# Second block's attention scores: split and stacked halves through DRAM in place of 64-row fp32

## The reference, cut to what matters

```python
# fox: 8 heads of width 64, causal, with a cumulative forget term
logits = einsum('bhqd,bhkd->bhqk', qi, k) / sqrt(64) + ci[..., :, None] - c[..., None, :]
logits = where(kpos <= qpos, logits, -inf);  out = softmax(logits) @ v

# differential: 4 heads, each with two maps of width 64; q and k are rotated first (rope)
p = softmax(where(kpos <= qpos, q_m k_m^T / sqrt(64), -inf))   # m = 0, 1
out = (p[0] - lam * p[1]) @ v                                   # v has width 128
```

## Time and profile before

| | us |
|---|---|
| median of 3 runs (lowest, highest) | 2890.78 (2885.82, 2891.13) |
| profiled execution, its time | 2890.61 |
| profiled execution, its span | 2888.9 |
| PE busy | 2612.1 (90% of the span) |
| DVE, ACT, POOL busy | 1001.0, 722.6, 708.0 |
| mean granted PE clock | 0.942 |

### The profile page before, as it was taken

How to read it: one execution, slowest core, us unless ns; L and a number is a source line. 1 busy time by engine, 2 the same in 40 slices (tenths; PEclk the granted TensorE clock), 3 DMA queues, 4 the chain that set the end, 5 groups by cost and what they waited for, 6 DMA issues and landing times. The chain is left out here.

```text
span 2888.9 us, 32486 instructions
## 1 busy us (share of the span) xinstructions
PE 2612.1 (90%) x12846; PEld 2094.6 (73%) x12846; DVE 1001.0 (35%) x1466; ACT 722.6 (25%) x1057; POOL 708.0 (25%) x437
## 2 busy tenths in 40 slices
PE   5899997599739899999999989899999989996987
PEld 4677776599737688888888768577777766674876
DVE  4055524444343521312213340122322314555523
ACT  3134454122111210201001210343432014443012
POOL 2111113133323233433333312111101221110221
PEclk9999998699869899999999989899999999998998
DMA  4411111222221111111111113011102111112422
GB/s 159 88 33 37 37 38 57 53 68 61 74 73 43 38 50 51 44 51 51 44 51 51 36 37 109 24 44 44 45 30 95 38 31 44 44 44 73 146 72 89
DMA packets 229584, 165.92 MB, mean 57 GB/s; under 512 B 40081, under 2 KB 212919, under 8 KB 228704
## 3 DMA queue, kind: packets, MB, share of 16 engines
q1 hardware_dynamic: 217888, 135.01, 16.6%
q10 hardware_dynamic: 11584, 29.36, 2.8%
HBM read 125.50 MB, written 38.85 MB: 57 GB/s over the span
## 5 line engine op out<-in xcount | busy, mean ns | idle before, releaser
L253 POOL CAST Wh<-Wraw 128x1024 fp32r<-128x1024 f32 x155 | 162.8, 1050 | 1784.9 <-PE PS L301 772.3
L255 POOL TENSOR_TENSOR Wl<-Wraw,Wh 128x1024 fp32r<-128x1024 f32 x155 | 399.3, 2576 | 22.3
L282 PE MATMUL PS<-XAh,Wh 128*128 128x512 f32 x520 | 165.7, 400 | 8.3 <-POOL Wl L255 4.2
L282 PE MATMUL PS<-XAl,Wh 128*128 128x512 f32 x520 | 161.5, 392 | 0.0
L282 PE MATMUL PS<-XAh,Wl 128*128 128x512 f32 x520 | 161.0, 391 | 0.0
L282 PE MATMUL PS<-XBl,Wh 128*128 128x512 f32 x520 | 160.1, 389 | 0.0
L282 PE MATMUL PS<-XBh,Wh 128*128 128x512 f32 x520 | 160.1, 389 | 0.0
L282 PE MATMUL PS<-XBh,Wl 128*128 128x512 f32 x520 | 160.0, 389 | 0.0
L282 PE MATMUL PS<-Fh,Wh 128*128 128x512 f32 x512 | 157.6, 389 | 0.0
L282 PE MATMUL PS<-Fl,Wh 128*128 128x512 f32 x512 | 157.6, 389 | 0.0
L282 PE MATMUL PS<-Fh,Wl 128*128 128x512 f32 x512 | 157.6, 389 | 0.0
(11 more groups left out here) (377 smaller groups left out, 5065.3 us busy)
## 6 DMA issues: line engine op xcount, KB each, us to landing
Wraw<-in_w_in SPq DMA_DIRECT2D x67, 512.0 KB, 4.0
Wraw<-in_w_ffn_in SPq DMA_DIRECT2D x32, 512.0 KB, 4.1
Wraw<-in_w_ffn_out SPq DMA_DIRECT2D x32, 512.0 KB, 3.9
x_scr<-hT SPq DMA_DIRECT2D x2, 4096.0 KB, 12.9
Wraw<-in_w_out SPq DMA_DIRECT2D x16, 512.0 KB, 4.6
gate_scr<-gbuf ACTq DMA_DIRECT2D x16, 512.0 KB, 2.6
gin<-gate_scr ACTq DMA_DIRECT2D x8, 1024.0 KB, 7.3
xtok<-in_x SPq DMA_DIRECT2D x4, 1024.0 KB, 8.6
```

Source lines behind the costliest of these rows:

```text
L253: pool.tensor_copy(Wh[:, slot], Wraw[:, slot])
L255: pool.tensor_tensor(Wl[:, slot], Wraw[:, slot], Wh[:, slot].bitcast(F32), ALU.subtract).then_inc(w_ready, 1)
L282: mm = pe.matmul(PS[:, 2 * slot + b, :], w[:, slot, k], x[:, b * 512:(b + 1) * 512], start=(c == 0 and m == 0), stop=(c == len(xs) - 1 and ...
```

## The change

The query of each head is split in a high and a low half, which are stacked on 128 rows (high on rows 0 to 63, low on 64 to 127). The key is split too, and each half is duplicated on both row groups. Two fp32r matmuls replace the fp32 one: stacked query times key-high, and stacked query times key-low. The halves are moved between partitions by a store to DRAM and a load from it.

```diff
+        st_h, st_l = sb("st_h", [P, 2, S], F32R, R + 48), sb("st_l", [P, 2, S], F32R, R + 56)
+        qs_scr, ks_scr = dram("qs_scr", [2, 4, P, S]), dram("ks_scr", [2, 4, P, S])
+        def store_halves(eng, j, hi, lo, out_sem):
+            scr = qs_scr if j < 4 else ks_scr
+            eng.dma_start(scr[0, j % 4], hi.bitcast(F32)).then_inc(out_sem, 16)
+            eng.dma_start(scr[1, j % 4], lo.bitcast(F32)).then_inc(out_sem, 16)
+        def load_map(eng, g, bufs, in_sem):
+            at = g * HD * S
+            q, kh, kl = bufs
+            eng.dma_start(q[:].bitcast(F32), bass.AP(qs_scr.tensor, at, [[4 * P * S, 2], [S, HD], [1, S]])).then_inc(in_sem, 16)
+            eng.dma_start(kh[:].bitcast(F32), bass.AP(ks_scr.tensor, at, [[0, 2], [S, HD], [1, S]])).then_inc(in_sem, 16)
+            eng.dma_start(kl[:].bitcast(F32), bass.AP(ks_scr.tensor, at + 4 * P * S, [[0, 2], [S, HD], [1, S]])).then_inc(in_sem, 16)
+        def map_scores(pe, bufs, i, dst):
+            q, kh, kl = bufs
+            for c, w in pieces(i):
+                for x in (kh, kl):
+                    mm = pe.matmul(dst(c)[:, 0:w * P], q[:, i * P:(i + 1) * P], x[:, c * 512:c * 512 + w * P],
+                                   start=(x is kh), stop=(x is kl and c != i // 4))
+            return pe.matmul(dst(c)[:, (w - 1) * P:w * P], identb[:], diagb[:], start=False, stop=True)
...
 act_phase9, for each of the 13 tiles:
-                if j < 12:
-                    act.activation((Qa, Ka, VaT)[j // 4][:, j % 4], pair(n % 2), ACT.Copy, scale=-0.125 if j < 4 else 1.0
-                                   ).then_inc(ps_free, 1)
+                if j < 8:
+                    if j >= 2:
+                        act.wait_ge(qk_out[j % 2], 32 * (j // 2))
+                    act.activation(st_h[:, j % 2], pair(n % 2), ACT.Copy, scale=-0.125 if j < 4 else 1.0).then_inc(qk_hi, 1)
+                    act.wait_ge(qk_hi, j + 1)
+                    act.wait_ge(qk_lo, j + 1)
+                    store_halves(act, j, st_h[:, j % 2], st_l[:, j % 2], qk_out[j % 2])
...
 dve_phase9, after ms_done 4:
-            for k in range(KT):
-                ins = dve.scalar_tensor_tensor(hT[:, k], hT[:, k], pv[:, V_FIN + k:V_FIN + k + 1], pair(2), ALU.mult, ALU.mult)
-            ins.then_inc(h_final, 1)
+            for j in range(8):
+                dve.wait_ge(qk_hi, j + 1)
+                dve.scalar_tensor_tensor(st_l[:, j % 2], pair((N_FOX + j) % 2), -0.125 if j < 4 else 1.0,
+                                         st_h[:, j % 2].bitcast(F32), ALU.mult, ALU.subtract).then_inc(qk_lo, 1)
+                dve.wait_ge(qk_lo, j + 1)
+                dve.sem_inc(ps_free, 1)
+                for k in (2 * j, 2 * j + 1):
+                    if k < KT:
+                        ins = dve.scalar_tensor_tensor(hT[:, k], hT[:, k], pv[:, V_FIN + k:V_FIN + k + 1], pair(2),
+                                                       ALU.mult, ALU.mult)
+                if j == 3:
+                    ins.then_inc(h_final, 1)
...
 sp_phase10: waits for qk_out, and behind the two constants:
+            for h in range(2):
+                load_map(sp, h, fox_bufs[h], qk_in[h])
...
 sp_phase11 (sp_phase14 likewise, with b_s and load_head):
-            load_range(sp, N_ZA + 2, N_QB + 2)
+            todo = [((i - 1) * FOX_STEPS / len(FOX_FILL), "tile", N_ZA + 2 + i) for i in range(len(FOX_FILL))]
+            todo += [(FOX_STEPS * (h - 1) / H8, "head", h) for h in range(2, H8)]
+            for _, what, x in sorted(todo):
+                if what == "tile":
+                    load_range(sp, x, x + 1)
+                else:
+                    sp.wait_ge(f_s, NT * (x - 1))
+                    load_map(sp, x, fox_bufs[x % 2], qk_in[x % 2])
...
 pe_phase11, scores(u) (pe_phase14 likewise, for each of the two maps):
+                if i == 0:
+                    pe.wait_ge(qk_in[h % 2], 48 * (h // 2 + 1))
...
+                map_scores(pe, fox_bufs[h % 2], i, lambda c: PS[:, 2 + 2 * (u % 2) + c]).then_inc(f_s, 1)
...
 act_phase12, after the copy of group g to xt, and once more at the end:
+            def high(g):
+                act.wait_ge(r_done, g + 1)
+                if g >= 2:
+                    act.wait_ge(rq_out[g % 2], 32 * (g // 2))
+                act.activation(rt_h[:, g % 2], rr[:, g % 2], ACT.Copy).then_inc(rq_hi, 1)
+                act.wait_ge(rq_hi, g + 1)
+                act.wait_ge(rq_lo, g + 1)
+                store_halves(act, g, rt_h[:, g % 2], rt_l[:, g % 2], rq_out[g % 2])
...
+                if g:
+                    high(g - 1)
+                if g == 4:
+                    act.wait_ge(o_y, 4)
+                    act.dma_start(ya_scr, Ya[:]).then_inc(ya_out, 16)
...
 dve_phase12, per group:
+                dve.wait_ge(rq_hi, g + 1)
+                dve.tensor_tensor(rt_l[:, g % 2], dst, rt_h[:, g % 2].bitcast(F32), ALU.subtract).then_inc(rq_lo, 1)
...
 sp_phase13, behind the four small loads:
+            for h in range(2):
+                load_head(sp, h)
...
 sp_phase15, behind the load of zt:
+            sp.dma_start(Ya[:], ya_scr).then_inc(ya_in, 16)
+            sp.wait_ge(ya_in, 16)
```

More of the change, by code:

```diff
@@ L1514, in dve_phase7, with map_bufs @@
                     dve.drain()
-        Qa, Ka = sb("Qa", [P, 4, S], F32, R), sb("Ka", [P, 4, S], F32, R + 16)
+        st_h, st_l = sb("st_h", [P, 2, S], F32R, R + 48), sb("st_l", [P, 2, S], F32R, R + 56)
+        qs_scr, ks_scr = dram("qs_scr", [2, 4, P, S]), dram("ks_scr", [2, 4, P, S])
+        qk_hi, qk_lo = late_sem("qk_hi"), late_sem("qk_lo")
+        qk_out, qk_in = [[late_sem(f"qk_{x}{i}") for i in range(2)] for x in ("out", "in")]
+        def store_halves(eng, j, hi, lo, out_sem):
[8 more added lines that the diff above has]
+            eng.dma_start(kl[:].bitcast(F32), bass.AP(ks_scr.tensor, at + 4 * P * S, [[0, 2], [S, HD], [1, S]])).then_inc(in_sem, 16)
+        def map_bufs(name, at):
+            return [sb(f"{name}_{x}", [P, S], F32R, at + 4 * i) for i, x in enumerate(("q", "kh", "kl"))]
+        def map_scores(pe, bufs, i, dst):
[5 more added lines that the diff above has]
+            return pe.matmul(dst(c)[:, (w - 1) * P:w * P], identb[:], diagb[:], start=False, stop=True)
         VaT = sb("VaT", [P, 4, S], F32, R + 32)
@@ L1557, in act_phase9 @@
                 act.wait_ge(mm_done, n + 1)
-                if j < 12:
-                    act.activation((Qa, Ka, VaT)[j // 4][:, j % 4], pair(n % 2), ACT.Copy, scale=-0.125 if j < 4 else 1.0
-                                   ).then_inc(ps_free, 1)
+                if j < 8:
[5 more added lines that the diff above has]
+                    store_halves(act, j, st_h[:, j % 2], st_l[:, j % 2], qk_out[j % 2])
+                elif j < 12:
+                    if j == 8:
+                        act.wait_ge(ps_free, N_FOX + 8)
+                    act.activation(VaT[:, j % 4], pair(n % 2), ACT.Copy).then_inc(ps_free, 1)
                 else:
@@ L1585, in dve_phase9 @@
             dve.wait_ge(ms_done, 4)
-            for k in range(KT):
-                ins = dve.scalar_tensor_tensor(hT[:, k], hT[:, k], pv[:, V_FIN + k:V_FIN + k + 1], pair(2), ALU.mult, ALU.mult)
-            ins.then_inc(h_final, 1)
+            for j in range(8):
[10 more added lines that the diff above has]
+                    ins.then_inc(h_final, 1)
+        fox_bufs = [map_bufs("fox0", R), map_bufs("fox1", R + 12)]
         vtok = sb("vtok", [P, NT, 512], F32, 0)
@@ L1599, in sp_phase10 @@
         def sp_phase10(sp):
+            for i in range(2):
+                sp.wait_ge(qk_out[i], 128)
             sp.dma_start(sel[:], a["consts"][0:H8, C_SEL:C_SEL + H8 * P]).then_inc(sel_in, 16)
             sp.dma_start(diagf[:], a["consts"][:, C_DIAG:C_DIAG + P]).then_inc(sel_in, 16)
+            for h in range(2):
+                load_map(sp, h, fox_bufs[h], qk_in[h])
             sp.wait_ge(sel_in, 32)
@@ L1689, in scores @@
                 h, i = divmod(u, NT)
-                r = slice(HD * (h % 2), HD * (h % 2) + HD)
+                if i == 0:
+                    pe.wait_ge(qk_in[h % 2], 48 * (h // 2 + 1))
                 if u >= 2:
                     pe.wait_ge(f_red, u - 1)
[L1693 to L1698, removed]
+                map_scores(pe, fox_bufs[h % 2], i, lambda c: PS[:, 2 + 2 * (u % 2) + c]).then_inc(f_s, 1)
             def turn(u, c, w, spreads):
@@ L1814, in build @@
         Ya = sb("Ya", [P, 4, S], F32, R)
-        Qb = sb("Qb", [P, 4, S], F32, R + 16)
-        Kb = sb("Kb", [P, 4, S], F32, R + 32)
+        rr = sb("rr", [P, 2, S], F32, R + 16)
+        rt_h, rt_l = sb("rt_h", [P, 2, S], F32R, R + 24), sb("rt_l", [P, 2, S], F32R, R + 32)
+        ya_scr = dram("ya_scr", [P, 4, S])
+        rq_hi, rq_lo, ya_out, ya_in = [late_sem(x) for x in ("rope_hi", "rope_lo", "ya_out", "ya_in")]
+        rq_out, rq_in = [[late_sem(f"rope_{x}{i}") for i in range(2)] for x in ("out", "in")]
         VbT = sb("VbT", [P, 4, S], F32, R + 48)
```

(27 more changed lines are left out.)

## The result

| | before | after |
|---|---|---|
| median of the runs on one chip (lowest, highest) | 2890.54 (2885.82, 2891.13) | 2957.43 (2955.49, 2964.05) |
| ratio, 95% interval | | 1.0236 [1.0218, 1.0254] |
| span of the profiled execution | 2888.9 | 2956.1 |
| mean granted PE clock | 0.942 | 0.918 |

The account below looks back on a forecast made before the run. PE was taken to bound both attention stretches. Columns 52 + fixed part 6 + clock 3 - first fox tile 0.7 - differential maps 1 - loop waits 2 = 57 us saved; 2890.6 - 57 = 2833 us, range 2810 to 2858.

Parts of the forecast that it names:

- Differential maps: Map loads ahead of the differential attention: head 0 landed at 2383.5, before the first score at 2385.38; 1 us lost.
- Fox maps: Map loads ahead of and within the fox attention: they land in time or have time to spare; nothing lost.
- The maps come late: Rival at the start of the differential stage: maps land late, 11 us more, 2844 us; chance 0.05.
- exposed weight loads: Slower rival in the scores: each of 384 new matmuls pays its weight load's 0.19 us, 2907 us; chance 0.06.
- Columns, 52: Scores of both attention stages: fp32r pairs cost less per piece than fp32, 3.26 us a map, 16 maps, 52 us saved.
- Fixed part, 6: The 0.21 us before each mask in both attention stages, 128 times: mostly remains, 0.05 saved each, 6 us.
- Clock, 3: Granted PE clock in the fox stage, where 14.8 us are lost: 3 us come back.
- First fox tile, 0.7: First tile of fox queries and keys: PE starts at 1708.5 instead of 1707.85, 0.7 us lost.
- Rotary stage, nothing: Rotary stage: a fourth DVE pass and ACT's high half take 2.3 of 8.3 us DVE idle; nothing lost.
- Gated output back, nothing: Load of the gated output, 2 MB behind `zt`: 13 us within a stretch of 20 us; nothing lost.
- Loop waits, 2: Attention loops: score groups get shorter while DVE and ACT work as before; 2 us of PE waiting.

Follow-up runs that it names:

- rows-outermost kernel: The changed kernel with the 64 rows, instead of the pair, as outer DRAM dimension of the map loads; 2793.18 us, 0.9664 of the kernel before.
- staging alone: The changed kernel's splits, stores and loads, in 64-row DMAs, but scores as 64-row fp32 matmuls on the high halves; 2898.23 us, 1.0021 of the kernel before.

## Why the prediction was wrong, step by step

**The step that failed: "Differential maps".** It said "head 0 is 3 MB, between the two DMA rows some 10.4 us: landed at 2383.5" and took 1 us. Twelve such loads held SP for 100.7 us (2355.54 to 2456.20). The 7.8 and 12.9 us of the earlier trace rows belong to transfers with 128 rows outermost, and I gave their rate to loads whose DRAM side has 2 outermost, an access pattern that stands in the diff. Megabytes were priced, not the shape. A second slip stands beside it: I asked when the data of head 0 land, and not when SP reaches the barrier, for which it must have issued both heads. "Fox maps", costed at nothing, is the same step: 25 us. Inside the differential stage the same loads and the weight loads behind them cost 40 us, of which 34.0 are PE's two waits for maps.

**The rivals.** "The maps come late" named the right place, with 11 us instead of 88 and a chance of 0.05; "exposed weight loads", the slower rival, did not happen: the starts in the group of 512 columns are 0.32 and 0.23 us apart.

**Columns, 52.** Right. Narrow pieces of 256 and 384 cost what I took, those of 128 less: in the 128 group above, 0.15 us to the second matmul (of which 0.09 is what the first start after another group takes in these rows, 0.32 against 0.23 at 512) and 0.11 to the mask, so 0.17 for the pair, where I had 0.23. In the rows-outermost kernel's timeline one of 256 takes 0.12, one of 384 0.17 to 0.18:
```profile
1900.37 0.28 PE L1544 MATMUL PS<-fox_kh,fox_q 128*128 128x256 f32 x1
1900.48 0.28 PE L1544 MATMUL PS<-fox_kl,fox_q 128*128 128x256 f32 x1
```
By these a map saves 6 x 0.39 + 2 x 0.29 + 2 x 0.19 + 2 x 0.04 = 3.38 us, all of them 54.

**Fixed part, 6.** Mis-sized. I thought that it belonged to the mask. It goes with the fp32 group: 0.12 us ahead of such a group (0.93 to 0.81 for the eight value matmuls) and 0.12 within it, 0.21 before and 0.09 now. 0.24 x 128 = 31 us, an estimate from two places in the fox stage; the 27 that I had named as the far end, and left, was nearer. The prediction also called the stretched first fp32r start one "after fp32"; what stands before it in the earlier trace rows is the bf16 mask.

**Clock, 3.** The fox stage has 0.99 in the rows-outermost kernel against 0.96: about 0.03 x 371 = 11 us. That the cheaper scores brought this is not shown: the kernel with the staging alone has 0.99 there too in its profile, with fp32 scores. What sets it stays open.

54 + 31 + 11 = 96 us; the rows-outermost kernel gained 97 in time, 53 in the fox stage and 43 in the differential one. The three terms are estimates from rows that fit their sum. Columns and fixed part give 27 + 15.5 us for each stage, and at nearly the same clock (0.99 and 0.98 to 0.99) the scores alone brought 43 in each (Staging alone); how these 43 divide between the two terms is argued, not measured.

**First fox tile, 0.7.** Right: PE waits 1.38 us where it waited 0.77. **Rotary stage, nothing.** Right; the fourth pass (L1971) waits 1.13 us for ACT's high half, and DVE still idles 5.9 us ahead of the next group:
```profile
2259.65 1.23 DVE L1971 TENSOR_TENSOR rt_l<-rr,rt_h 128x1024 fp32r<-128x1024 f32 x1 [1.13 <-ACT rt_h L1930]
2266.79 1.22 DVE L1966 TENSOR_TENSOR rt<-PS,sinT 128x1024 f32<-128x1024 f32 x1 [5.92 <-PE PS L1920]
```
**Gated output back, nothing.** 21.0 us against 20. **Loop waits, 2.** 0.7 us for an exponential in the rows-outermost kernel.

What I did not look for at all: a cheaper way to the same gain. The two maps of a differential head stood on different halves of the rows, one mask apart.

## What to carry to other kernels

Price a DMA by the slowest dimension of its access pattern, before its bytes: with a pair or a repeat outermost it has two engines and 51 GB/s here, with the rows outermost over 240. Where a stage ends in a barrier, a queue that only issues is on the path as soon as its issues block; ask when the last issue ends, not when the first data land. And before 64-row fp32 matmuls are rebuilt, look at what stands between those on different halves of the rows.

## What the runs showed that I had not expected

A queue takes two such loads at once and blocks at whatever load comes third; another queue does not help, since the loads share the same engines (19.6 us a load instead of 9.8, and 2971 against 2957 us). Two 64-row fp32 matmuls on rows 0 to 63 and 64 to 127 run in the time of one (0.64 us for 256 columns and both maps), if they are issued next to each other; one bf16 matmul on all 128 rows between them doubles it. An fp32 group among fp32r matmuls cost some 0.24 us beyond its columns where I read it, an estimate that fits the 43 us of each stage.
